# Banded attention: two of a unit's four heads scaled by their reciprocal sums on GpSimd instead of VectorE

## What is computed

```python
s = jnp.einsum('bnqkgd,bnjkd->bnkgqj', qb, kb).astype(jnp.float32) * (Dh ** -0.5)
s = s - slopes[:, :, None, None] * dist.astype(jnp.float32)
s = jnp.where(mask[None, :, None, None], s, -jnp.inf)
m = jnp.maximum(s.max(axis=-1), sink)
p = jnp.exp(s - m[..., None])
denom = p.sum(axis=-1) + jnp.exp(sink - m)
p = (p / denom[..., None]).astype(vb.dtype)
o = jnp.einsum('bnkgqj,bnjkd->bnqkgd', p, vb).reshape(B, S, Hq * Dh)
```

## Time and profile before

| | |
|---|---|
| runs | 3022.16 to 3023.38 us, median 3023.01 |
| profiled execution | 3022.8 us |
| its span | 3021.0 us |
| PE busy | 2909.4 us (96%) |
| DVE busy | 1661.0 us (55%) |
| ACT busy | 720.5 us (24%) |
| POOL busy | 74.6 us (2%) |

### The profile page before, as it was taken

How to read it: one execution, slowest core, us unless ns; L and a number is a source line. 1 busy time by engine, 2 the same in 40 slices (tenths; PEclk the granted TensorE clock), 3 DMA queues, 4 the chain that set the end, 5 groups by cost and what they waited for, 6 DMA issues and landing times.

```text
span 3021.0 us, 36256 instructions
## 1 busy us (share of the span) xinstructions
PE 2909.4 (96%) x14418; PEld 2183.9 (72%) x14418; DVE 1661.0 (55%) x2731; ACT 720.5 (24%) x1394; POOL 74.6 (2%) x138
## 2 busy tenths in 40 slices
PE   7999999999899999979999999999999998999998
PEld 5988988788557888844444434578888846888887
DVE  4787788265666677631111157464555468655555
ACT  3444444220573101111011123420000116200001
POOL 0000000000000101000000001000000020000000
PEclk9999999999999999989999999999999999999999
DMA  5100111121102556279999977012222271122221
GB/s 237 70 36 35 49 57 49 42 91 56 67 12 98 194 186 223 108 326 421 422 422 422 422 298 320 29 56 84 84 84 84 112 273 36 56 84 89 102 89 56
DMA packets 71735, 451.73 MB, mean 150 GB/s; under 512 B 8016, under 2 KB 10208, under 8 KB 24096
## 3 DMA queue, kind: packets, MB, share of 16 engines
q1 hardware_dynamic: 53824, 374.17, 30.9%
q0 software_dynamic: 17040, 73.18, 6.7%
q10 hardware_dynamic: 720, 2.29, 0.2%
HBM read 445.41 MB, written 2.10 MB: 148 GB/s over the span
## 4 chain that ended last, share of the span: by engine, by line
PE 84%; DVE 8%; DMA 3%; DVEq 2%; ACT 2%; issue 1%; ACTq 0%; SPq 0%
PE PS L253 78%; PE PS L1706 1%; DMA ring<-stream 1%; PE PS L1589 1%; DVE arena L1656 1%; PE PS L1689 1%; DVE stat L1715 1%; DVEq L1155 1%; DMA hT<-stream 1%; PE PS L2490 1%; DMA arena<-x 0%; DVE PS L2844 0%; PE PS L2470 0%; DVE arena L1151 0%; DVE arena L1176 0%
## 5 line engine op out<-in xcount | busy, mean ns | idle before, releaser
L253 PE MATMUL PS<-arena 128*128 128x256 f32 (+3 forms) x4960 | 982.6, 388 | 21.4 <-DVE arena L1193 8.6
L253 PEld LDWEIGHTS PS<-arena 128*128 128x128 f32 (+1 forms) x4960 | 742.5, 183 | 237.5 <-issue 152.0
L253 PE MATMUL PS<-arena,ring 128*128 128x256 f32 (+1 forms) x1992 | 466.9, 390 | 0.0
L253 PEld LDWEIGHTS PS<-arena,ring 128*128 128x128 f32 x1992 | 377.8, 190 | 73.8 <-issue 25.5
L253 PE MATMUL PS<-hT,ring 128*128 128x256 f32 (+1 forms) x1504 | 403.3, 423 | 8.5 <-ACT hT L348 4.4
L253 PEld LDWEIGHTS PS<-hT,ring 128*128 128x128 f32 x1504 | 285.6, 191 | 113.0 <-issue 79.6
L253 PE MATMUL PS<-xT,arena 128*128 128x256 f32 x1056 | 232.4, 379 | 0.0
L253 PEld LDWEIGHTS PS<-xT,arena 128*128 128x128 f32 x1056 | 200.5, 190 | 31.4 <-issue 4.8
L2239 DVE TENSOR_TENSOR arena<-arena,PS 128x512 f32<-128x512 f32 x16 | 11.0, 687 | 369.4 <-PE PS L253 369.4
L253 PE MATMUL PS<-hT,arena 128*128 128x256 f32 (+1 forms) x864 | 195.1, 442 | 0.8 <-DMA hT<-stream 0.8
L628 DVE CUSTOM_DVE_ANT_0 arena<-arena,PS 128x1024 f32<-128x1024 f32 x128 | 151.9, 1218 | 43.3 <-DMA arena<-adat 41.7
(11 more groups left out here) (317 smaller groups left out, 3022.5 us busy)
## 6 DMA issues: line engine op xcount, KB each, us to landing
ring<-stream SPq DMA_DIRECT2D x217, 1024.0 KB, 7.0
arena<-stream SPq DMA_DIRECT2D x98, 1024.0 KB, 18.4
arena<-adat POOLq DMA_DIRECT2D x88, 512.0 KB, 5.0
hT<-stream SPq DMA_DIRECT2D x32, 1024.0 KB, 18.7
arena<-adat POOLq DMA_DIRECT2D x20, 1024.0 KB, 10.6
arena<-stream SPq DMA_DIRECT2D x8, 512.0 KB, 4.4
arena<-x ACTq DMA_DIRECT2D x4, 512.0 KB, 15.4
xT<-stream SPq DMA_DIRECT2D x2, 1024.0 KB, 20.8
```

The costliest lines, as they stand in the source:

```text
L253: ins = nc.tensor.matmul(out_, lhsT, rhs, start=start, stop=stop_, **kw)
```

## The change

VectorE multiplies only heads 0 and 1 of a unit of the banded attention. GpSimd gets a new program, `pool_`, which waits for the reciprocals (semaphore `a_r`), multiplies heads 2 and 3 in one tensor_tensor whose second input is the two reciprocals broadcast along the keys, and signals `a_h`. It stands behind the value bias in GpSimd's order. TensorE's first two heads wait for `a_n` as before; the transposes of half c = 1 also wait for `a_h`. The other two attentions keep all their heads on VectorE. Besides, the three attentions now share one set of semaphores, each counting on from where the one before ended (u0, i0 and o0 are the offsets); which instruction waits for which is unchanged by that.

```diff
-        def attention(name, n, nh, score, chunk, dest, groups, value, outs, exp_io, norm_io, maximum, scale,
+        a_s, a_m, a_e, a_n, a_t, a_c, a_v, a_o, a_r, a_h = (sem(f"att_{x}") for x in
+            ("s", "m", "e", "n", "t", "c", "v", "o", "r", "h"))
+
+        def attention(u0, i0, o0, n, nh, score, chunk, dest, groups, value, outs, exp_io, norm_io, maximum, scale,
...
-                    pe.wait_ge(a_n, u + 1)
+                    pe.wait_ge(a_n, u0 + u + 1)
                     for c in range(2):
+                        if sink and c:
+                            pe.wait_ge(a_h, u + 1)
                         if u >= 1:
-                            pe.wait_ge(a_c, 2 * (u - 1) + c + 1)
+                            pe.wait_ge(a_c, 2 * u0 + 2 * (u - 1) + c + 1)
...
-                    nc.vector.reciprocal(col(RECIP, u), col(SUM, u))
+                    recip = nc.vector.reciprocal(col(RECIP, u), col(SUM, u))
+                    if sink:
+                        recip.then_inc(a_r, 1)
                     v.drain()
-                    for h in range(nh):
+                    for h in range(nh // 2 if sink else nh):
                         x = norm_io(u, h)
                         ins = nc.vector.tensor_scalar(x, x, col(RECIP, u)[:, h:h + 1], None, ALU.mult)
                     ins.then_inc(a_n, 1)
...
-            return pe_, act_, dve_, a_o, a_s
+            def pool_(pool):
+                for u in range(n):
+                    pool.wait_ge(a_r, u + 1)
+                    x = norm_io(u, slice(nh // 2, nh))
+                    nc.gpsimd.tensor_tensor(x, x, col(RECIP, u)[:, nh // 2:nh].unsqueeze(2).broadcast_to(
+                        [P, nh // 2, x.shape[2]]), ALU.mult).then_inc(a_h, 1)
+
+            return pe_, act_, dve_, pool_
...
-        swa_att_pe, swa_att_act, swa_att_dve, swa_out, _ = attention(
-            "swa", 16, 4, swa_score, swa_chunk, swa_dest, [[u] for u in range(16)], swa_value,
+        swa_att_pe, swa_att_act, swa_att_dve, swa_att_pool = attention(
+            80, 20, 16, 16, 4, swa_score, swa_chunk, swa_dest, [[u] for u in range(16)], swa_value,
...
             swa_bias_pool(pool)
+            swa_att_pool(pool)
```

More of the change, by code:

```diff
@@ L1529, in keys_dve, with swap_halves @@
             ins.then_inc(kp_ok, 1)
-        def swap_halves(pool, gqa_scores):
+        def swap_halves(pool):
             for j in range(KT):
@@ L1535, in swap_halves @@
                 if j >= 2:
-                    pool.wait_ge(gqa_scores, 8 * (j - 1))
+                    pool.wait_ge(a_s, 8 * (j - 1))
                 elif j == 0:
@@ L1566, in scores @@
                     if u >= 2:
-                        pe.wait_ge(a_e, u - 1)
+                        pe.wait_ge(a_e, u0 + u - 1)
                     score(u, S2[u % 2]).then_inc(a_s, 1)
                 def values(i):
-                    pe.wait_ge(a_c, 2 * last_unit[i] + 2)
+                    pe.wait_ge(a_c, 2 * u0 + 2 * last_unit[i] + 2)
                     busy = [j for j in range(i) if outs(j) and value(None, j) == value(None, i)]
                     if busy:
-                        pe.wait_ge(a_o, out_count[busy[-1] + 1])
+                        pe.wait_ge(a_o, o0 + out_count[busy[-1] + 1])
                     value(pe, i).then_inc(a_v, 1)
@@ L1599, in exps @@
                 def exps(u):
-                    act.wait_ge(a_m, u + 1)
+                    act.wait_ge(a_m, u0 + u + 1)
                     if u >= 2:
-                        act.wait_ge(a_t, 2 * (u - 2) + 2)
+                        act.wait_ge(a_t, 2 * u0 + 2 * (u - 2) + 2)
                     if sink:
@@ L1613, in copies @@
                     if i >= 2 and u == groups[i][0]:
-                        act.wait_ge(a_v, i - 1)
+                        act.wait_ge(a_v, i0 + i - 1)
                     for c in range(2):
-                        act.wait_ge(a_t, 2 * u + c + 1)
+                        act.wait_ge(a_t, 2 * u0 + 2 * u + c + 1)
                         dst, src = dest(u, c, TB[c])
@@ L1715, in gqa_maximum @@
             return nc.vector.tensor_reduce(neg, S[:, :, 0:HK], AX.XY, ALU.max, negate=True)
-        gqa_pe, gqa_act, gqa_dve, gqa_out, gqa_scores = attention(
-            "gqa", 64, 1, gqa_score, gqa_chunk, gqa_dest, [list(range(4 * i, 4 * i + 4)) for i in range(16)],
+        gqa_pe, gqa_act, gqa_dve, _ = attention(
+            0, 0, 0, 64, 1, gqa_score, gqa_chunk, gqa_dest, [list(range(4 * i, 4 * i + 4)) for i in range(16)],
             gqa_value, gqa_outs, lambda u, h, S: (Pb[:, u % 2, :, :], S[:, :, 0:HK]),
@@ L1742, in quad_parts @@
                 elif n == N_MERGE + 7 and i == 3:
-                    pe.wait_ge(gqa_out, 8)
+                    pe.wait_ge(a_o, 8)
                     mod_sum(pe, 1)
@@ L2501, in mla_maximum @@
             return nc.vector.tensor_scalar(neg, top, -float((NOPE + ROPE_D) ** -0.5), None, ALU.mult)
-        mla_att_pe, mla_att_act, mla_att_dve, mla_out, _ = attention(
-            "mla", 16, 2, mla_score, mla_chunk, mla_dest, [list(range(4 * i, 4 * i + 4)) for i in range(4)],
+        mla_att_pe, mla_att_act, mla_att_dve, _ = attention(
+            64, 16, 8, 16, 2, mla_score, mla_chunk, mla_dest, [list(range(4 * i, 4 * i + 4)) for i in range(4)],
             mla_value, lambda it: [(qn[:, 2 * it + c, :], OB2[c]) for c in range(2)],
@@ L3030, in _ @@
             sums_dve(v, N_MWO)
-            v.wait_ge(mla_out, 8)
+            v.wait_ge(a_o, 16)
             block_sums(v, qn, T_w)
@@ L3040, in _ @@
             sums_dve(v, N_SWO)
-            v.wait_ge(swa_out, 8)
+            v.wait_ge(a_o, 24)
             block_sums(v, qn, T_w)
```

16 lines of the change are left out of this document (7 added, 9 removed).

## The result

The changed kernel takes 3025.74 us (median of 20 runs, 3023.56 to 3028.82) against 3020.99 us for the kernel before (20 runs, 3019.47 to 3024.06): a ratio of 1.0013, 95% interval 1.0007 to 1.0019, that is 2 to 6 us more. It is slower, but by less than the 0.2% that the prediction set as its bound. Its profiled execution took 3023.73 us, with a span of 3021.9 us.

A forecast was written before the change was run, and what follows sets the result against it. Two nearly equal paths, VectorE's own and one through TensorE, bound the banded attention. 12 wide units at 0.51 and 3 narrow at 0.14 give 6.5 us; less 0.5 and 0.7, +5.3 on 3022.8: 3028 us, range 3026 to 3030.

The forecast's parts named there:

- no change by 0.2%: Whole kernel: time stays within the 6.0 us that a measurement can tell, 3022.8 us before; chance 0.67.
- The two paths: Banded attention: VectorE alone, 3.57 us a unit, and a path through TensorE, 3.47 each, set the pace; both must shorten.
- The case of no collision: Rival: VectorE and GpSimd do not hinder each other, ScalarE then bounds, -4 us to 3019 us; chance 0.13.
- The collision: VectorE's scalings and GpSimd's multiplication exclude each other at shared SBUF ports; wide units 0.51 us longer, narrow ones 0.14.
- GpSimd slips in between: Forecast case: GpSimd runs between VectorE's two scalings, next peak at +1.64 us instead of +1.13 in wide units; chance 0.35.
- slower rival: GpSimd starts after the first scaling ends, or before both; wide units 0.83 us longer, +9.9 us, 3033 us; chance 0.22.
- GpSimd's length: GpSimd's multiplication of two heads: 1.27 us in a wide unit, as the value bias, and 0.70 in a narrow one.
- Both bounds, 0.63 and 1.9: GpSimd's wide multiplication: 0.63 us if its repeated input need not be read again, 1.9 if it is read badly.
- "Nothing" for the shared semaphores: Shared semaphores and TensorE's added wait instruction: no cost counted, 0.05 us a unit, 0.8 in all, as upper bound.
- Nothing for unit 0's place behind the value bias: Unit 0's GpSimd part queues behind the second value bias; scores at about 2514.2 us, needed at 2514.4: no cost.
- VectorE keeps both: Rival: VectorE holds the ports through both scalings and GpSimd starts at +0.69 us; -1.5 us, 3021 us; chance 0.26.
- The sign that was named: Profile rows: one scaling about 1.3 us, the other 0.35, GpSimd 1.27, and 3.9 to 4.0 us a unit.

The follow-up runs named there:

- experiments 2 and 3: Changed kernel with heads 2 and 3 unscaled: without any GpSimd work 3019.30 us; with GpSimd multiplying other data at the same moment 3025.05 us.
- experiment 5: Changed kernel with VectorE's two scalings also adding up what they write, to move one column at a time: 3021.20 us, attention stretch 53.69 us.
- experiment 6: Changed kernel with one, three or five one-column GpSimd memsets in front of its multiplication: 3028.00, 3024.52 (one run) and 3024.49 us (one run).
- three memsets: Changed kernel with three one-column GpSimd memsets in front of its multiplication, which then starts 0.09 us behind the first scaling's start: 3024.52 us (one run).
- experiment 4: Changed kernel with GpSimd waiting for VectorE's second scaling instead of the reciprocal: 3022.14 us, attention stretch 54.35 us.

## Why the prediction was right, point by point

The forecast was 3028 us, 5.3 us more, with "no change by 0.2%" as the likeliest outcome; measured were 3025.74 us, 4.7 us more in the runs and 2.65 us in the stretch. The outcome was the one forecast, and the cause, GpSimd holding up a scaling in each unit, was the one named. That 4.7 comes so near to 5.3 is in part luck: the stretch, which is what the sum was about, moved by half of it, and 3025.74 lies just under the forecast's own range of 3026 to 3030.

- **The two paths and what bounds them** held. Taking two scalings away without company gave 3.5 us, where VectorE alone would have given 8.0, because other work takes over: four units took 12.87 us, and in them ScalarE was busy for 11.91 and VectorE for 10.56. The case of no collision was priced at 4.
- **The collision** held and is the whole of the result: the same kernel with and without GpSimd's operation beside it is 58.2 against 52.0 us (experiments 2 and 3), and with scalings that take one column at a time it is 53.7 (experiment 5).
- **"GpSimd slips in between"** failed as a description of this kernel. GpSimd comes before both scalings, 0.01 us ahead, and stops the first. The prediction named that order only in passing, under its slower rival, without a sum of its own. As a rule of the ports the step was right: once GpSimd comes 0.09 us or more after the first scaling, it does go between the two (experiment 6). For a wide unit the two orders differ by little, since either way one scaling waits out GpSimd: the next peak is at +1.45 here, and at 2531.63 - 2530.22 = +1.41 with three memsets.
- **GpSimd's length, the term that was mis-sized.** It was taken from the value bias, 1.27 us for 512 columns; the scaling takes 1.04. For 256 columns it is 0.61, where 0.70 was taken. Why it is shorter no run tells: the second input repeats one number along the columns instead of a row, and the operation is a multiplication instead of an addition. In the forecast's own sum, 0.23 us less in 12 wide units and 0.09 in 3 narrow ones is 3.0 us; the reversed order gives back 0.04 us in each wide one (+1.45 against 0.11 + 1.04 + 0.26 = +1.41), 0.5 in all. 5.3 - 3.0 + 0.5 = 2.8; 2.65 was measured. Both bounds, 0.63 and 1.9, were far off.
- **"Nothing" for the shared semaphores** held inside the attention (55.54 against 55.56 us), and for the whole time within 2.7 us. **Nothing for unit 0's place behind the value bias** held: TensorE waits 0.99 us for GpSimd there, and the peak of unit 3 does not wait for the scores.
- **VectorE keeps both** is refuted by experiment 6; the version that orders it so by a semaphore (experiment 4) gains 1.2 us of the stretch where 1.5 had been worked out for it.
- The sign that was named, one of two scalings near 1.3 us and 3.9 to 4.0 us a unit, came out as 1.17 and 14.68 / 4 = 3.67: the right picture at the smaller size.

## What to carry to other kernels

Before work is moved from VectorE to GpSimd, look whether VectorE's instructions beside it move two columns at a time between SBUF and SBUF: these and GpSimd's exclude each other, and a 0.35 us instruction can wait out the whole 1.04 us. Let GpSimd start behind them, beside work in PSUM, or write them in a form that takes one column at a time. They are not the only ones: an operation of 4 columns with two inputs in SBUF was held too, 0.68 us instead of 0.16. And price the move by the stretch without the moved work at all (here 3.5 us of 55.6): where the second path is within 0.1 us a unit of the first, that is far less than the sum of what is taken away.

## What the runs showed of the hardware that I had not expected

- GpSimd's two-input operation took 1.04 us for 512 columns with a broadcast second input, 0.61 for 256 and 0.40 for 128, and 1.27 us for the value bias, an addition of 512 columns whose second input repeats a row of 256. Which of the two differences is worth the fifth was not tested.
- Which of two engines gets the ports is not always told by their recorded starts. GpSimd was let in first at 0.02 us behind VectorE's first scaling, second at 0.09.
- A tensor_scalar that also accumulates took 0.48 us instead of 0.35 for 256 columns, its read of the accumulator 0.08, where that of the peak takes 0.14.
